# Residual-stream loads placed behind the first weight pieces: one fused two-layer forward pass

## The reference

```python
# first block: h has 16 extra "meta" tokens in front
h = h + rmsnorm(z @ w_out[l], mix_norm_post[l])              # stage_project, then stage_add_norm
u = rmsnorm(h, ffn_norm_pre[l])
gt = causal_dwconv(u @ ffn_w_gate[l], ffn_conv_w[l], ffn_conv_b[l])
y = (gelu(gt) * (u @ ffn_w_up[l])) @ ffn_w_down[l]           # stage_down
h = h + rmsnorm(y, ffn_norm_post[l])                         # stage_add_norm
# second block
x = x + concatenate([att, hm], axis=-1) @ w_out[l]           # stage_residual "wo2"
x = x + memory_cross_attention(...)                          # its last product: stage_residual "wc", no load of h
x = x + hierarchical_moe(...)                                # 32 experts, top 2
```

## Time and profile before

| what | us |
|---|---|
| median of the three runs | 3313.31 |
| the profiled execution, own time | 3310.01 |
| its span in the trace | 3308.3 |
| TensorE busy (matmul) | 2809.9, 85% of the span |
| VectorE busy | 1619.6, 49% |
| ScalarE busy | 1210.2, 37% |
| GpSimd busy | 590.2, 18% |
| mean granted clock of TensorE, share of full | 0.921 |

### The profile page before, as it was taken

How to read it: one execution, slowest core, us unless ns; L and a number is a source line. 1 busy time by engine, 2 the same in 40 slices (tenths; PEclk the granted TensorE clock), 3 DMA queues, 4 the chain that set the end, 5 groups by cost and what they waited for, 6 DMA issues and landing times. The chain is left out here.

```text
span 3308.3 us, 38889 instructions
## 1 busy us (share of the span) xinstructions
PE 2809.9 (85%) x14587; PEld 2444.1 (74%) x14587; DVE 1619.6 (49%) x1963; ACT 1210.2 (37%) x1741; POOL 590.2 (18%) x340
## 2 busy tenths in 40 slices
PE   4889999897679999979975998978667489999992
PEld 2879999797568999868755887657556468888882
DVE  2336655361433323323443613752332479999995
ACT  3223333331221111112332314642222167777773
POOL 2000000002322222200121000003201324444441
PEclk7999999998889999989987999999888589999996
DMA  2333323243111111122211111112002179999995
GB/s 104 103 103 104 103 90 93 106 122 102 51 51 45 51 44 48 41 108 95 95 67 61 45 51 58 52 51 58 26 0 94 67 299 412 401 408 406 406 403 201
DMA packets 224435, 432.14 MB, mean 131 GB/s; under 512 B 21586, under 2 KB 162242, under 8 KB 198994
## 3 DMA queue, kind: packets, MB, share of 16 engines
q1 hardware_dynamic: 214322, 396.21, 33.5%
q0 software_dynamic: 10016, 34.62, 2.6%
HBM read 370.85 MB, written 59.93 MB: 130 GB/s over the span
## 5 line engine op out<-in xcount | busy, mean ns | idle before, releaser
L3121 DVE TENSOR_TENSOR k_w_lo<-k_raw,k_w_hi 128x2048 fp32r<-128x2048 f32 x192 | 435.2, 2290 | 50.9 <-ACT k_w_hi L3067 47.0
L3067 ACT CAST k_w_hi<-k_raw 128x2048 fp32r<-128x2048 f32 x192 | 363.6, 1908 | 94.9 <-PE bank L2987 48.0
L198 PE MATMUL bank<-u_ffn_hi,f_w_hi 128*128 128x342 f32 (+1 forms) x880 | 308.3, 350 | 33.7 <-POOL f_w_lo L1342 33.7
L199 PE MATMUL bank<-u_ffn_lo,f_w_hi 128*128 128x342 f32 (+1 forms) x880 | 308.2, 350 | 0.0
L200 PE MATMUL bank<-u_ffn_hi,f_w_lo 128*128 128x342 f32 (+1 forms) x880 | 307.9, 350 | 0.0
L257 POOL TENSOR_TENSOR wo_w_lo<-wo_w,wo_w_hi 128x1024 fp32r<-128x1024 f32 x16 | 39.3, 2460 | 1049.4 <-ACT wo_w_hi L253 1049.4
L2985 PE MATMUL bank<-k_w_hi,k_x_hi 128*128 128x512 f32 x512 | 206.3, 403 | 5.8 <-DVE k_x_lo L3127 5.5
L198 PEld LDWEIGHTS bank<-u_ffn_hi,f_w_hi 128*128 128x128 f32 x880 | 166.7, 189 | 49.9 <-issue 34.2
L198 PE MATMUL bank<-u_hi,g_w_hi 128*128 128x342 f32 (+2 forms) x576 | 191.7, 333 | 13.8 <-DVE g_w_lo L765 10.8
L2986 PE MATMUL bank<-k_w_lo,k_x_hi 128*128 128x512 f32 x512 | 203.2, 397 | 0.0
L2987 PE MATMUL bank<-k_w_hi,k_x_lo 128*128 128x512 f32 x512 | 203.0, 397 | 0.0
(11 more groups left out here) (533 smaller groups left out, 6829.4 us busy)
## 6 DMA issues: line engine op xcount, KB each, us to landing
k_raw<-in_w_e_gate_dram SPq DMA_DIRECT2D x64, 1024.0 KB, 8.2
k_raw<-in_w_e_up_dram SPq DMA_DIRECT2D x64, 1024.0 KB, 7.5
k_raw<-in_w_e_down_dram SPq DMA_DIRECT2D x64, 1024.0 KB, 8.2
d_raw<-in_ffn_w_down_dram SPq DMA_DIRECT2D x44, 512.0 KB, 3.2
g_w<-in_w_in_dram SPq DMA_DIRECT2D x24, 512.0 KB, 4.1
f_raw<-in_ffn_w_gate_dram SPq DMA_DIRECT2D x22, 512.0 KB, 3.8
f_raw<-in_ffn_w_up_dram SPq DMA_DIRECT2D x22, 512.0 KB, 3.8
gate_scratch<-g_out SPq DMA_DIRECT2D x20, 513.0 KB, 6.5
```

The source lines that it names most:

```text
L198: pe.matmul(out, wh[:, t, :], xh[t][:, c:c + n], start=t == 0, stop=False)
L199: pe.matmul(out, wh[:, t, :], xl[t][:, c:c + n], start=False, stop=False)
L3067: act.copy(wh[:, q, :], raw[:, r, :]).then_inc(hi_made, 1)
L3121: dve.tensor_tensor(wl[:, q, :], raw[:, r, :], wh[:, q, :], ALU.subtract).then_inc(lo_made, 1)
```

## The change

In wo1 the load of `h` is cut into eight parts, one for each tile of 128 features. Part n is issued right behind weight piece n, with two semaphores in turn; the loop of SP is written out. In the down product the one load of `h` stands behind all 22 weight loads of the first half and ahead of the first weight load of the second half. In wo2 it stands behind the first two weight pieces. Nothing else is altered, and no other engine's instructions change.

```diff
 def stage_project(...):
-    mm, kept, squared, added, h_in = sems(ctx, nc, name, "mm kept squared added h_in")
+    mm, kept, squared, added, h_in0, h_in1 = sems(ctx, nc, name, "mm kept squared added h_in0 h_in1")
+    h_in = (h_in0, h_in1)
...
         def _(sp):
-            sp.dma_start(h[:, :, :], h_load).then_inc(h_in, 16)
-            with sp.Fori(0, KD // 2) as i:
-                for s in range(2):
-                    wt.load(sp, 2 * i + s, s, w[:, :, ds((2 * i + s) * P, P)])
-            sp.wait_ge(h_in, 16)
+            for n in range(KD):
+                s = n % 2
+                wt.load(sp, n, s, w[:, :, n * P:(n + 1) * P])
+                if n >= 2:
+                    sp.wait_ge(h_in[s], 16 * (n // 2))
+                sp.dma_start(h[:, n, :], h_load[:, n, :]).then_inc(h_in[s], 16)
+            for s in range(2):
+                sp.wait_ge(h_in[s], 8 * KD)
 def stage_down(...):
         def _(sp):
-            sp.dma_start(h[:, :, :], h_load).then_inc(h_in, 16)
             for half in range(2):
                 with sp.Fori(0, PAIRS_K) as i:
                     for s in range(2):
                         sp.wait_ge(lo_made, free(KF * half + 2 * i + s))
                         sp.dma_start(raw[:, s, :], w[ds((2 * i + s) * P, P), :]).then_inc(w_in[s], 16)
+                if half == 0:
+                    sp.dma_start(h[:, :, :], h_load).then_inc(h_in, 16)
             sp.wait_ge(h_in, 16)
 def stage_residual(...):
         def _(sp):
-            if h_load is not None:
-                sp.dma_start(h[:, :, :], h_load).then_inc(h_in, 16)
-            with sp.Fori(0, KD // 2) as i:
+            def pair(i):
                 for s in range(2):
                     at = ds((2 * i + s) * P, P)
                     wt.load(sp, 2 * i + s, s, weights[:, at] if gains else w[:, :, at])
+            pair(0)
+            if h_load is not None:
+                sp.dma_start(h[:, :, :], h_load).then_inc(h_in, 16)
+            with sp.Fori(1, KD // 2) as i:
+                pair(i)
```

## The result

The changed kernel takes 3288.78 us (median of 4 runs, 3283.61 to 3290.84). The kernel before, run beside it, takes 3313.02 us (4 runs, 3310.92 to 3319.05). The ratio, formed over all runs and not over the two medians, is 0.9921, with an interval of 0.9907 to 0.9935: faster by 24.2 us. The forecast was 3280.0 us, so the time lies 8.8 us above it, just inside the end of the range at 3289. The profiled execution took 3287.87 us itself and has a span of 3286.1 us, 22.2 us less than before.

A forecast was written before the change was run, and what follows sets the result against it. TensorE, 85% busy, was taken as the bound, idling at three stage starts behind the load of h. Gains 11.4 + 12.5 + 11.2 − 1.8 = 33.3 us took 3310.0 to 3276.7, plus 3.3 to the median: 3280.0 us, range 3272 to 3289.

The forecast's parts named there:

- C: Stage starts: first transfer is late whatever it is, starts gain nothing, the boundary's 1.8 us remains; 3315 us, chance 0.03.
- D: Down product, half two: boundary stall leaves TensorE at 1.2 GHz throughout, costing 110 us; 3390 us, chance 0.02.
- B: wo2: VectorE's first addition or piece 2 becomes the new wait, price 5.4 us; 3285 us, chance 0.07.
- A: Down product's boundary of halves: idle times bring TensorE's clock down, price 1.8 to 3.1 us; 3282.5 us, chance 0.14.
- wo1's start: Start of wo1: weight piece 0 lands 3.8 us after issue, gain 11.4 us, bounds 10.4 to 11.6.
- Down product's start: Start of the down product: weight piece 0 lands 3.2 us after issue, gain 12.5 us, bounds 11.7 to 12.9.
- wo2's start: Start of wo2: the weight piece's third DMA lands at 2228.1, gain 11.2 us, bounds 10.3 to 11.5.
- Boundary: Between the down product's halves: first piece of half two 4.3 us late, net loss 1.8 us, bounds nothing to 6.
- Clock of TensorE: Slow clock behind long idle times at wo1's and the down product's starts: unchanged, nothing; bounds +2.3 to −1.2 us.
- The sum: Whole kernel: three starts' gains less the boundary's loss, 11.4 + 12.5 + 11.2 − 1.8 = 33.3 us.
- The rule that gave 28.9 us: Three starts: 2.0 us plus bytes at 436 GB/s per DMA, 9.6 us saved each, boundary free; weighed but not used.
- From profile to median: Whole kernel: median lies 3.3 us above the profiled execution, difference kept, turning 3276.7 into 3280.0 us.

The follow-up runs named there:

- g_first: Changed kernel with half of the down product's h load at the boundary, half behind its last piece, plus a 2 KB load awaited before weight piece 0; 3279.08 us.
- e_wo1: Kernel before with only the first output projection (wo1) changed; 3303.96 us, ratio 0.9967.
- e_wo2: Kernel before with only the second output projection (wo2) changed; 3305.54 us, ratio 0.9973.
- f_half: Changed kernel with half of the down product's h load between the halves, the other half behind the last weight piece; 3280.25 us, ratio 0.9904.
- g_half: Repeat of the kernel with the down product's h load split between the boundary and behind the last weight piece; 3281.35 us, ratio 0.9904.
- f_alone: Changed kernel with the down product's h load behind its last weight piece, and piece 1 issued only once piece 0 has landed; 3279.95 us, ratio 0.9897.
- g_pool: Changed kernel with the down product's h load split in halves; in wo2 GpSimd's second low weight part waits for VectorE's activation parts; 3280.89 us.

## Why the prediction was right, and where it fell short

The mechanism was right: all three starts waited for weight piece 0 behind the stream, and the wait went. Rivals C and D fell at once. B fell too: in wo2 VectorE waits for TensorE. A came true in part: the clock fell at the boundary, but the lost time lies mostly elsewhere. By the forecast's own steps:

- **wo1's start**: forecast 11.4 us; ScalarE's first high part comes 11.3 us earlier (766.75 − 755.42), and behind the stage's slow beginning 10.5 to 11.1 us of it remain in the table. Right.
- **Down product's start**: forecast 12.5 us, bounds 11.7 to 12.9; TensorE's idle time fell by 10.7 us only (20.98 to 10.30). The term for the landing was mis-sized: 3.2 us taken, 4.9 us found, because of the instruction fetch (g_first shows it). The table's 11.6 to 12.1 look better by luck. They hold 1.3 to 1.8 us that e_wo1 and e_wo2 win as well, with the old wait: the 6.1 us at 1.2 GHz behind it in the profile of before are the longest of all profiles, the others have 3.0 to 3.8 us. The change itself is worth some 10.4 us here.
- **wo2's start**: forecast 11.2 us, measured 10.6 to 11.2. Right.
- **Boundary**: forecast −1.8 us. Beside the kernels without the whole stream there (−1.6), the changed kernel's profiles lose 1.1 to 2.0 us more (−2.7, −3.6, −3.4), so the size was right. Its make-up was not. The stream took 16.4 us, not 14.5, and the first piece of half two landed 18.1 us after its predecessor's issue (at about 1532.8), not 17.1. ScalarE was 5.4 us late instead of 4.3: half one ends 22.5 us earlier than before, 1550.9 against 1573.4, the high part only 17.1 us earlier. TensorE then stood for 4.26 us in one piece and lost the clock, as rival A had it (0.63 in the stretch above). What paid for that was the old idle time of 2.45 us, which vanished.
- **Clock of TensorE, the step that failed**: "put it at nothing". I weighed only the clock behind the long idle times at the starts. The shorter idle times (2.45 us at the boundary, 2.90 us at the input projection) stood in the profile of before with the full clock behind them, and I took that as a property of the places. At the boundary it was one draw of nine. Against the profile of before the changed kernel's loses 2.6 us at the input projection, 3.6 in the mixers and 1.6 in wo2, 7.8 us in all. The first and the last are in all three profiles of the changed kernel and are its price: 4.2 to 5.2 us that the forecast put at nothing. The mixers' part comes and goes in one and the same kernel (0.1 to −3.6 in its three profiles) and stands in e_wo2 too, whose program up to there is that of before; it is no price of the change.
- **The sum**: starts 33.9 (10.8 + 11.9 + 11.2) − 2.7 − 2.6 − 3.6 − 1.6 = 23.4 us; the remaining stretches make −1.2 us, and the last ScalarE instruction comes 22.2 us earlier. Measured against e_wo1 and e_wo2 where they run the old code, the changed kernel's three profiles give 25 to 27 us, an estimate from the table: the starts without the 1.5 us that the down product wins anyway (32 us), less 1.1 to 2.0 at the boundary, 2.6 to 3.6 at the input projection and 1.6 in wo2. The rule that gave 28.9 us was nearer to the three medians (24.2, 27.9 and 27.1 us), but for another reason: its 9.6 us a start are refuted by the rows of all three.
- **From profile to median**: I kept the 3.3 us between the profile of before and its median. For the changed kernel the median lies 0.9 us above its profile, and in the repeats −1.1 and 0.0 us. The profile of before was a fast draw of its kernel, so part of the gain that its rows promised was luck already spent. e_wo1 and e_wo2 bear this out for the boundary (1.6 us) and e_wo2 for the mixers (3.6 us), less the 1.3 to 1.8 us at the down product's start. That the whole difference between profile and median comes from such places is an inference.

What stays open: why a given idle time is followed by a fall in one kernel and not in another. Pure chance doesn't fit, since the input projection went 4 of 4 and 0 of 9. A fixed rule of the idle time's length doesn't fit either, since 2.90 us did both. For wo2 the rows of f_half and g_half show the step before it, but not why the clock comes back sooner in one execution than in the other. What TensorE did before the idle time was not varied by itself.

The best versions here, f_alone, f_half, g_first and g_pool, take 3279.1 to 3281 us, at ratios of 0.990 to 0.991 to the kernel before. They lie 4 to 7 us below the changed kernel's medians of 3285.4 and 3286.3 us, which is less than the 0.3% that a measurement of this kernel can tell. f_half is the plainest of them.

## What to carry to other kernels

A large transfer that nothing in its stage needs belongs behind the first pieces of the weights, and in portions small enough for the time that covers each: half of it at the boundary cost nothing, all of it 1 to 2 us there and in its four profiles another 2.4 to 3.6 us at the input projection. Where TensorE is the bound, split its change in time into idle and busy at the same count of instructions before explaining a gain: here idle fell by 35.1 us and busy rose by 12.9. Do it against more than one profile of the old kernel, or against kernels that still run the old code in the stage: a good part of those 12.9 us was the old profile's luck. Treat every idle time like those of 2.3 us and more below in an old profile as one that may bring the clock down in the next version, even where its own profile shows the full clock, and take gains from medians rather than from two profiles.

## What the hardware showed unexpectedly

- Idle times of TensorE of 2.33 to 2.34 us (wo2), 2.45 to 2.50 us (boundary) and 2.90 us (input projection) were followed by the clock of 1.2 GHz in 5 of 5, 8 of 9 and 4 of 13 profiles. In wo2 the profiles without a fall, that of before among them, had 1.11 to 1.45 us there, and g_pool 0.17.
- An earlier return to 2.4 GHz can cost time: in wo2 it made the next wait 2.33 us instead of 1.11, and the clock fell again (g_half against f_half).
- One instruction fetch of 16 KB on one DMA engine went with a 512 KB piece used 4.8 to 5.2 us after its issue in the nine profiles where piece 0 leads the stage and the fetch runs beside it, and 3.4 us in g_first, where the fetch came ahead.
- VectorE's subtraction of 128x1024 takes 1.21 us alone, and 3.38 us for the one that meets GpSimd's.
